# Hybrid decoder step on one core: two blocks of the cross-attention part made into one, padded queries made earlier, bias loads moved between the key loads

## What is computed

```python
def layer_tail(h, mem_k, mem_v, norm_x, w_xq, w_xo, norm_ffn, ...):
    h = h + cross_attend(rms_norm(h, norm_x), mem_k, mem_v, w_xq, w_xo)
    return h + moe_ffn(rms_norm(h, norm_ffn), w_router, b_router, w_e1, b_e1, w_e2, b_e2)

def prompt_layer(...):
    ...                                   # gated DeltaNet heads and latent attention heads
    h = x + jnp.concatenate([y_gdn, y_mla], axis=-1) @ w_out
    mem_k, mem_v = memory_kv(mem, mem_norm, w_xk, w_xv)   # 256 memory tokens, 4 heads x 256
    y = layer_tail(h, mem_k, mem_v, ...)

def sample_layer(...):                    # the same, with cached mem_k, mem_v of 8 sequences
    ...

def cross_attend(hn, mem_k, mem_v, w_xq, w_xo):
    q = (hn @ w_xq).reshape(B, T, 4, 256)
    s = jnp.einsum('bthd,bmhd->bhtm', q, mem_k) * 256 ** -0.5
    p = jax.nn.softmax(s, axis=-1)
    return jnp.einsum('bhtm,bmhd->bthd', p, mem_v).reshape(B, T, 1024) @ w_xo
```

## Time and profile before

| | |
|---|---|
| median of 3 runs | 1510.64 us |
| time of the profiled execution | 1512.73 us |
| its span in the profile | 1510.7 us |
| PE busy | 1395.6 us (92%) |
| DVE, ACT, POOL busy | 461.6, 237.4, 42.5 us |
| mean DMA rate | 325 GB/s |
| mean granted TensorE clock | 0.957 of full speed |

### The profile page before, as it was taken

The page is one execution under the profiler, slowest core; times in us unless marked ns, Lnnn a source line. Parts: engine busy times, 40 slices in busy tenths (PEclk is TensorE's granted clock), DMA queues, the critical chain, the costliest instruction groups (busy, mean ns, idle before and its releaser), DMA issues.

```text
span 1510.7 us, 21293 instructions
## 1 busy us (share of the span) xinstructions
PE 1395.6 (92%) x8579; PEld 692.9 (46%) x8579; DVE 461.6 (31%) x1124; ACT 237.4 (16%) x420; POOL 42.5 (3%) x37
## 2 busy tenths in 40 slices
PE   8999899898998989999999989989889899899896
PEld 7668766554476553333333333333333333333332
DVE  1856643542114253113112211221221122113213
ACT  1053232321012450100100100000000001001002
POOL 0000110000000330000000000000000000000000
PEclk9999999799999989999999999999999999999999
DMA  9111534348364567999999999999999999999996
GB/s 363 39 61 49 202 142 183 140 166 308 139 251 120 204 265 328 428 425 424 427 424 425 427 425 425 425 424 428 425 423 427 424 425 427 424 425 425 424 426 249
DMA packets 96724, 490.69 MB, mean 325 GB/s; under 512 B 9307, under 2 KB 14527, under 8 KB 61626
## 3 DMA queue, kind: packets, MB, share of 16 engines
q1 hardware_dynamic: 94074, 468.89, 75.8%
q0 software_dynamic: 2304, 20.97, 3.6%
q10 hardware_dynamic: 296, 0.11, 0.0%
HBM read 484.01 MB, written 6.04 MB: 324 GB/s over the span
## 4 chain that ended last, share of the span: by engine, by line
PE 41%; DMA 17%; DVE 6%; issue 2%; ACT 1%; SPq 1%; POOL 1%; DVEq 0%
DMA arena<-in_w_e 16%; PE ps L1985 15%; PE ps L2021 15%; PE ps L2033 4%; PE ps L1975 2%; PE ps L2008 1%; DVE arena L2553 1%; DVE arena L2563 1%; DVE arena L2560 1%; DVE arena L2561 1%; DMA arena<-in_cache_mem_k 1%; PE ps L2063 1%; PE ps L2049 1%; SPq L1632 1%; PE ps L2037 1%
## 5 line engine op out<-in xcount | busy, mean ns | idle before, releaser
L1985 PE MATMUL ps<-arena 128*64 128x512 f32 x2048 | 454.5, 595 | 17.8 <-DMA arena<-in_w_e 17.2
L1985 PEld LDWEIGHTS ps<-arena 128*64 128x64 f32 x2048 | 145.3, 137 | 298.9 <-issue 297.5
L2021 PE MATMUL ps<-arena 128*64 128x512 f32 x960 | 227.5, 634 | 2.2 <-ACT arena L2235 2.0
L2021 PEld LDWEIGHTS ps<-arena 128*64 128x64 f32 x960 | 78.9, 147 | 148.7 <-issue 135.8
L2560 DVE TENSOR_SCALAR arena<-ps 128x1024 f32<-128x1024 f32 x15 | 18.4, 1225 | 292.9 <-PE ps L1985 292.9
L2572 DVE COPY arena<-ps 128x512 f32<-128x512 f32 x15 | 10.4, 692 | 229.9 <-PE ps L2021 229.9
L2233 ACT ACTIVATE arena<-arena 128x1024 f32<-128x1024 f32 x15 | 15.9, 1058 | 324.9 <-DVE arena L2560 324.9
L2578 DVE TENSOR_TENSOR res<-res,ps 128x512 f32<-128x512 f32 x60 | 41.3, 688 | 81.1 <-PE ps L2033 81.1
L2008 PE MATMUL ps<-cst,arena 128*128 128x128 f32 x120 | 21.7, 340 | 43.7 <-DVE arena L2553 43.7
L1661 PE MATMUL ps<-arena 128*128 128x512 f32 x128 | 57.5, 608 | 2.9 <-PEq L160 2.9
L1968 PEld LDWEIGHTS ps<-arena 128*128 128x128 bf16 x768 | 50.3, 100 | 14.0 <-issue 12.2
(11 more groups left out here) (552 smaller groups left out, 1548.9 us busy)
## 6 DMA issues: line engine op xcount, KB each, us to landing
arena<-in_w_e SPq DMA_DIRECT2D x384, 1024.0 KB, 17.8
arena<-in_w_in SPq DMA_DIRECT2D x8, 1380.0 KB, 17.7
arena<-in_cache_mem_k SPq DMA_DIRECT2D x8, 1024.0 KB, 10.4
arena<-in_w_out SPq DMA_DIRECT2D x2, 2048.0 KB
arena<-in_w_xk SPq DMA_DIRECT2D x1, 4096.0 KB, 16.1
arena<-in_w_xv SPq DMA_DIRECT2D x1, 4096.0 KB, 12.6
arena<-in_w_xq SPq DMA_DIRECT2D x1, 4096.0 KB, 23.3
arena<-in_cache_mem_v SPq DMA_DIRECT2D x1, 4096.0 KB, 16.3
```

The costliest lines, as they stand in the source:

```text
L1985: last = pe.matmul(ps[64 * x:64 * x + 64, c, :], xe[:, k, 64 * x:64 * x + 64], ring[n % RING][:, c * 512:(c + 1) * 512], start=False, stop ...
L2021: last = pe.matmul(ps[64 * x:64 * x + 64, 4 + c, :], aT[:, k, 64 * x:64 * x + 64], ring[(n + x) % RING][:, j * D + c * 512:j * D + (c + 1) ...
```

## The change

The sample-step block and the prompt block become one, with no barrier between them. What the barrier ordered is now ordered by three waits:

- PE waits before the first memory part until all four pieces of `memT` are out of PSUM (`mem_emptied`, 4), and before the transposes of the keys for `drained`, which DVE gives behind its last addition to `res`.
- ACT waits for `drained` before it squares `res`.
- SP waits for `mem_emptied` before its first expert load, `fill(0)`.

DVE's `take_out(0)` of the memory moves ahead of the wait for `x_loaded`. The padded queries are made at the end of the joint block: POOL clears `qpad` (at a place behind `KTx`) when all queries are made, and ACT copies the strips behind its last exponentials; PE's wait for `q_ready`, DVE's 8 copies and POOL's clearing leave the next block. The six bias loads leave their place ahead of the key loads; one pair is issued behind each of the key loads 1, 2 and 3.

The diff, without the code that only moved from one block into the other:

```diff
-    squares, factors, scale, turn, take_out, _ = norm_steps("mem", ..., banks=(0, 2))
+    squares, factors, scale, turn, take_out, mem_emptied = norm_steps("mem", ..., banks=(0, 2))
...
+    qpad = Arena(arena, AT_WXQ + 2 * KD * MEM).take([P, KD, DEC, 32])
...
             load_cross_weights(sp, n_stored[0])
+            sp.wait_ge(mem_emptied, 4)
+            fill(sp, 0, 0)
...
+            act.wait_ge(drained, 1)
+            x_squares(act)
...
             exps(3)
+            act.wait_ge(cx["padded"], 1)
+            for n in range(2 * H):
+                nc.scalar.copy(qpad[:, n].rearrange("p b c -> p (b c)")[:, 0:33 * (DEC - 1) + 1:33], qxT[:, n, SEQ:TOK])
...
             for k in range(STEP_HEAD, STEPS):
                 sampled_pool(pool, k)
+            pool.wait_ge(cx["q_made"], KD)
+            nc.gpsimd.memset(qpad, 0.0).then_inc(cx["padded"], 1)
...
             join_sum(dve)
+            take_out(dve, 0)
             dve.wait_ge(x_loaded, 32)
             for i, (t, n, bank) in enumerate(MIX):
...
                 if i == 1:
-                    take_out(dve, 0)
                     join_out(dve)
             take_out(dve, 1)
...
+            last.then_inc(drained, 1)
...
-    clear_semaphores()
-    with nc.Block() as block:
-        @block.sync
-        def _(sp):
-            fill(sp, 0, 0)
...
             pe.wait_ge(wk_loaded, 16)
+            pe.wait_ge(mem_emptied, 4)
             for i in range(8):
...
                 if c == 3:
+                    pe.wait_ge(drained, 1)
                     for j in range(4):
...
             sp.wait_ge(stored, memory_stored)
-            for i in range(3):
-                sp.dma_start(bias[i * NE:(i + 1) * NE, 0:2 * D], b_e1[0]).then_inc(mo["b_loaded"], 16)
-                sp.dma_start(bias[i * NE:(i + 1) * NE, 2 * D:3 * D], b_e2[0]).then_inc(mo["b_loaded"], 16)
             for b in range(G):
                 sp.wait_ge(sx["scored"], b + 1)
                 sp.dma_start(Kx[:, b], cache_mem_k[0, G + b].rearrange("(s p) h n -> p s (h n)", p=P)).then_inc(kx_loaded[b], 16)
+                if b > 0:
+                    part = slice((b - 1) * NE, b * NE)
+                    sp.dma_start(bias[part, 0:2 * D], b_e1[0]).then_inc(mo["b_loaded"], 16)
+                    sp.dma_start(bias[part, 2 * D:3 * D], b_e2[0]).then_inc(mo["b_loaded"], 16)
...
                 turn_keys(m)
-                if m == 2:
-                    pe.wait_ge(sx["q_ready"], 1)
...
-            nc.gpsimd.memset(qpad, 0.0).then_inc(sx["cleared"], 1)
...
             take_keys(0)
-            dve.wait_ge(sx["cleared"], 1)
-            for n in range(2 * H):
-                strip = qpad[:, n].rearrange("p b c -> p (b c)")[:, 0:33 * (DEC - 1) + 1:33]
-                last = nc.vector.tensor_copy(strip, qxT[:, n, SEQ:TOK])
-            last.then_inc(sx["q_ready"], 1)
```

More of the change, by code:

```diff
@@ new lines, in build @@
+    qxT = Arena(arena, AT_QX).take([P, KD, TOK])
+    oxT = xnT
+    G = 4
+    Kx = Arena(arena, AT_WK).take([P, G, 2, D])
+    Vx = Arena(arena, AT_WV).take([P, G, 2, D])
+    kx_loaded = [sem(f"xkey{b}_loaded", True) for b in range(G)]
+    vx_loaded = sem("xvalue_loaded", True)
+    x_squares, x_factors, x_scale, x_turn, x_take_out, x_emptied = norm_steps("x", res, (0, 1, 2), V_X, x_loaded, 32, AT_WOUT, banks=(6, 7))
+    RING = 12
+    AT_RING = (AT_MEMT, AT_WOUT, AT_MV, AT_MKT, *(AT_WK + 2048 * i for i in range(4)), *(AT_WV + 2048 * i for i in range(4)))
@@ new lines, in build, with fill @@
+    ring = [arena[:, at:at + 2048] for at in AT_RING]
+    full = [sem(f"ring{s}_full", True) for s in range(RING)]
+    free = [sem(f"ring{s}_free", True) for s in range(RING)]
+    FILLS = 24
+    def fill(sp, n, e):
+        s, x = n % RING, n % 2
+        if n < 16:
+            k = n // 2
+            src = w_e1[0, bass.ds(e + x, 1), k * P:(k + 1) * P, :].rearrange("a p n -> (a p) n")
+            sp.dma_start(ring[s], src).then_inc(full[s], 16)
+        else:
+            k = 2 * ((n - 16) // 2)
+            src = w_e2[0, bass.ds(e + x, 1), k * P:(k + 2) * P, :].rearrange("a (k p) n -> p (a k) n", p=P)
+            sp.dma_start(ring[s].rearrange("p (k n) -> p k n", k=2), src).then_inc(full[s], 16)
@@ L1429, in build @@
+    drained = sem("mix_drained")
     with nc.Block() as block:
@@ new lines, in out_moved @@
+            def out_moved(k):
+                dve.wait_ge(cx["out"], k + 1)
+                nc.vector.tensor_copy(oxT[:, k, 0:SEQ], ps[:, k, 0:SEQ]).then_inc(cx["out_moved"], 1)
+            negative_max(0)
+            negative_max(1)
+            probs(0)
+            negative_max(2)
+            probs(1)
+            probs(2)
+            negative_max(3)
+            probs_out(0)
+            probs_out(1)
+            probs(3)
+            probs_out(2)
+            for k in range(4):
+                out_moved(k)
@@ L1533, in _ @@
+            probs_out(3)
+            for k in range(4, KD):
+                out_moved(k)
         @block.tensor
@@ L1693, in _ @@
                 if i < NT:
-                    turn(pe, i)
+                    x_turn(pe, i)
             pe.wait_ge(wxq_loaded, 16)
@@ L1722, in _ @@
                 last.then_inc(cx["out"], 1)
[L1724 to L1747, removed]
```

141 lines of the change are left out of this document (69 added, 72 removed).

## The result

| | before | after |
|---|---|---|
| median | 1511.71 us (1509.61 to 1513.29, 6 runs) | 1501.48 us (1498.77 to 1504.84, 6 runs) |
| ratio | | 0.9933 [0.992, 0.9946] |
| profiled execution | 1512.73 us | 1499.03 us |
| its span | 1510.7 us | 1497.2 us |
| PE busy | 1395.6 us | 1385.4 us |

The change is faster by 0.67%.

What follows compares the result with a forecast made beforehand. The expert loop was taken as bound by its transfers, starting when PE arrives. Gains of 4.76, 4.55 and 3.58 us ahead of it sum to 12.9, giving a median of 1497.7 us, range 1492.5 to 1502.5.

Steps and rivals of the forecast that it cites:

- The moved take_out: Before the memory's second turn: 3.22 us of PE waiting goes, plus 1.54 from full clock, 4.76 in all.
- The barrier: Before the first memory part: 2.88 us idle goes, plus 1.77 from full clock, less 0.1, 4.55 in all.
- What was late next: Behind the first memory part: the norm of res loses its 3.5 us to spare; 0.1 us charged.
- The padded queries: Ahead of the first score: PE's wait goes, 0.5 us gained; the moved work is covered by 7.7 us.
- The bias loads: At the sample scores: 4.48 us wait and 2.5 slow clock go, less 2.3 new stall and 1.6 clock loss.
- S = 2p - 3.3 ... S = 2.3: PE's new stall at the eighth sequence's keys, with p the cost of a bias pair, 2.8 us.
- the forecast's slack: At the seventh sequence's keys: key load 2's data over at 488.5 without pairs, PE wanting it at 491.3.
- The charge for the clock: Behind the new stall in the sample scores: PE's clock falls, costing 1.6 us.
- No key load comes late: Rival, 25%: at the scores a pair costs 1.65 us or less, no stall or clock loss; gain 16.8, 1493.8 us.
- The clock does not come back: Rival, 15%: small multiplications around second turn and sample-row step cause low clock; 1.54 and 1.77 stay lost, 1501.0 us.
- The gain does not reach the end: Rival, 3%: expert loop's transfers do not start with PE's first freed slot, so its end stays; 1510.6 us.
- slower, by the queue: Rival, 3%: a key load waits for two bias pairs at 10.9 us each, stall 18.5; 1514.8 us.

Runs made afterwards that it cites:

- e6: The change with the two blocks kept apart and the barrier between them again: 1506.30 us, 0.9951 of the kernel before.
- e3: The change with the memory's first take_out again behind the wait for res: 1505.70 us, 0.996 of the kernel before.
- e5: The changed kernel itself run once more, nothing altered: 1500.10 us, 0.9906 of the kernel before.
- e7: The change with all three pairs of bias loads behind the second key load (key load 1): 1501.61 us, one run.
- e8: The change with all bias loads behind the fourth key load, repeated with more rounds: 1495.16 us, 0.9885 of the kernel before.
- e1: The change with all three pairs of bias loads behind the fourth key load: 1496.70 us, 0.9894 of the kernel before.
- e4: The change with the same bias bytes sent to 128 partitions in smaller pieces, not 32: 1496.32 us, 0.9883 of the kernel before.
- e2: The change with the six bias loads again ahead of all key loads: 1499.59 us, 0.9911 of the kernel before.

## Why the prediction was right, and which of its terms were not

**The bound.** Right. The loop takes the same 941 us behind its first multiplication, and the time moved with its start.

**The moved take_out.** The wait of 3.22 went, and turn and step take 7.87 against the 7.75 that was expected. But its price, if the `take_out` alone is moved, was put too low. e6 has the moved take_out without the joint block, and its M to T is 6.47 less than before: 3.22 + 1.42 + 0.16, and another 1.69, since the first memory part behind the barrier no longer ran slow. The forecast gave this term 4.76.

**The barrier.** The step that failed is "the clock is 0.51 a microsecond later": I took the 2.88 idle as the cause of the slow part behind it, and booked 1.77 for the barrier alone. e6 has the same idle time at the same place and no slow part (7.11). Nor is the earlier stall enough: e3 has it, longer (5.22), without the barrier, and no slow part either (7.13). Only the kernel before has both, and 8.80. So, as far as one trace of each tells, the slow part needed both, and either edit removes it.

The two terms are thus not independent of each other: the 1.7 goes with whichever edit comes first. The stretch from the sample-row step to the end of the first memory part is 15.16 before and 10.67 in e3, so as the first edit the barrier is worth 4.49 there, which is the 4.55; as the second it is worth 2.80 (13.47 in e6, 10.67 in the change), 2.18 with the last barrier taken off. Over all of M to T, e3 against before shows only 3.14, because the last barrier took 0.6 more and the stall with its slow stretch happened to be longer. The two edits together give what was summed for both (9.13 against 9.31). Nor does the bracket hold between 1.46 "after which it stayed at 1.00" and 2.88 "after which it fell" as a rule on the length of a gap: 2.88 did not make it fall in e6, nor 2.06 at the last barrier of the change, and 1.80 did in e5.

**What was late next.** The norm of `res` was said to come 0.1 late; it came with the end of the memory part. Not foreseen was the last barrier, 2.06 in place of 1.46, which took back 0.6. The rows of the line that clears semaphores, in the window around this barrier, first before, then after:

```profile
L159 POOLq DRAIN  x2: 66/68/71, 473.5 to 473.7; - x2
L159 POOLq EVENT_SEMAPHORE_RANGE_CLEAR  x2: 69/91/113, 473.6 to 473.8; - x2
```

```profile
L159 POOLq DRAIN  x4: 61/78/100, 462.9 to 463.7; - x4
L159 POOLq EVENT_SEMAPHORE_RANGE_CLEAR  x4: 67/111/178, 463.1 to 463.8; - x4
```

The joint block's semaphores are cleared in four ranges, each behind a drain, in 0.9 us; before it was two in 0.3, and the other two had been cleared at the barrier that is gone. PE's first work stands behind this barrier; in e6, which clears two ranges here again, its gap is back at 1.49.

**The padded queries.** Right: covered by 6 us, and worth 0.61 (T to the first score 3.54 before, 2.93 after) against 0.5. No run undoes this part alone.

**The bias loads.** The kind of the new wait was right, and its place in part: the forecast put it at the eighth's keys, "perhaps a shorter one" at the seventh's, and the seventh's is the longer one in e3 (1.84 and 1.54) and e6 (2.87 and 1.10) and the only one in e5. The term that was mis-sized is "S = 2p - 3.3 ... S = 2.3". S was 3.27 in the profiled change, which makes p 3.3, and 1.80 in e5, which makes it 2.55; e3 and e6, with the same order of loads, give 3.38 and 3.97. e7 gives 2.66. So 2.8 lies among the values, and the term has a spread of 2 us from run to run which one number does not show. But all of these take the forecast's slack as given, and that was too large: it counted the data of key load 2 over at 488.5, 2.8 ahead of PE, if no pair stood in the way, and e8 and e1 measure 1.3 and 1.0, since the load is only issued once its slot is free. At 2.8 a pair this makes a wait of 1.5 to 1.8 for the seventh's keys, where the forecast had none; the runs show 1.31 to 2.87. Read with the measured slack, a pair costs 2.1 to 2.2 in e7 and, from the seventh's wait behind one pair, 2.3 to 4.2. The charge for the clock, 1.6, was right: 0.66 on the transposes, 0.87 on the score and 0.05 on the transposes behind it. In the scores the forecast's 3.58 became 2.70: 0.61 + 4.48 + 2.5 - 3.27 - 1.6 = 2.72.

The Trainium skill (SBUF — State Buffer, section "Door 1: The DMA port swizzle") makes 32 partitions slow because they reach eight of 16 ports. e4 agrees with its direction: at 128 partitions, with smaller pieces, the stall falls to 0.32. By its half rate a pair would be an estimated 1.9 us; the runs put it at 2.1 to 4.2, so the measurement decides for more than that, by little in e7 and by much in e6.

**The rest** of the difference, 1.02 us, lies between the scores and the loop, where nothing was changed. Over all ten profiles this stretch takes 61.6 to 62.7, in the change 61.60 and in e5, the same kernel, 62.44. So it is no merit of the change, and what sets it was not looked into. It was luck for the sum: without it 11.35 us would have come of the 12.9.

**The rivals.** "No key load comes late" did not happen, but e8 shows what it is worth: M to loop 230.55, a gain of 16.6 against the 16.8 that was worked out. "The clock does not come back" fell for the places it named: 1.00 from 338 to 464. The time of 1501.0 that it gave happens to be near the median; the mechanism is not there. "The gain does not reach the end" and "slower, by the queue" fell with the loop's length and with p.

**The sum and the median.** From M on, 12.37 came of the 12.9 forecast. The medians differ by 10.2 in the first comparison and by 12.8 in e5's, with M spread over 4.6 us in the profiles. Of the 3.8 us by which the forecast lies below the first median, 0.5 is gain that did not come, 1.1 is the median of before, 1510.64 on three runs and 1511.71 on six, and the other 2.1 lie between the traced stretch (12.37) and the medians (10.2), probably in the spread; no trace shows them. The forecast's range is 0.3 to 0.5 wider than its own words give (1493.8 less 1, 1501.0 plus 1); the median lies in either.

## What to carry to other kernels

Where an engine is about to wait for wide loads, try putting the narrow ones (here 32 partitions) behind them all, not between them: here, spread out, they turned one wait of 3.43 us (e2) into one or two shorter ones of 1.80 to 3.97 together, with a loss of clock behind them still, and behind all keys they cost PE nothing. A slow stretch behind an idle one need not be that one's doing alone, so undo each of two neighbouring stalls by itself before booking the clock's loss to either. A load's slack runs from its own issue and landing, so look when it can be issued, and not only when the load ahead of it is through. Where executions differ ahead of the part in question, compare stretches between the same two instructions of each trace, not medians.

## What the runs showed of the hardware that was not expected

- The same narrow loads that leave the DMA share at 1.03 cut the rate from 398 to 312 GB/s; a share near 1 does not say that bytes move at the highest rate seen.
- PE's stretch of 32 small multiplications (L1367, 3.63 us) without any idle time around it is followed by a half clock for some 2 to 3 us in nine of the ten profiles, but not in e3, with the same instructions. The windows view of the change there:

```profile
330.30:334.50 4.20, 4.20 (x39) 4.20 (x38) 1.52 (x4) 0.00 (x0) 0.00 (x0) 0.97 1.00 390
334.80:337.50 2.70, 2.70 (x5) 1.16 (x4) 0.97 (x2) 0.00 (x0) 0.00 (x0) 0.50 1.06 350
```

  So the clock also fell where no idle time stood ahead, behind light work, as the forecast's second rival supposed for other places. That the light work is the cause is not shown, and what decides between e3 and the others stays open.
- Idle stretches of PE near 2 us do not have one outcome. In the scores 1.31 (change) and 1.54 (e3) left the clock at 1.00, and 1.80 (e5), 1.84 (e3), 1.96 (change) and 2.87 (e6) did not; at the barriers 2.06 (change) and 2.88 (e6) left it there too, and 2.88 (before, behind the earlier stall) did not.
- Why the same order of loads gives a stall of 1.80 in one execution of the change (e5) and of 3.27 in another was not tried, and stays open.
